# Mixer A's scores two tiles at a time, its values in the bank of turned q and k

## What is computed

```python
def diff_attention(q, k, v, lam):          # 4 heads, q and k of width 64 for each of 2 maps, v of width 128
    s = jnp.einsum('bhmqd,bhmkd->bhmqk', qb, k).astype(jnp.float32) * scale
    p = jax.nn.softmax(s, axis=-1)
    w = p[:, :, 0] - lam * p[:, :, 1]
    return jnp.einsum('bhqk,bhkd->bhqd', w.astype(v.dtype), v)
...
ya = diff_attention(qa, ka, va, lam)
ya = merge_heads(rms_norm(ya, subln_a) * (1.0 - lam_init))
```

## Time and profile before

| | |
|---|---|
| median of 3 runs | 2302.98 us (2302.33 to 2303.56) |
| profiled execution, first to last instruction | 2300.6 us |
| granted TensorE clock, mean | 0.999 |
| PE busy | 2263.2 us (98%) |
| PEld busy | 2125.2 us (92%) |
| DVE busy | 1720.5 us (75%) |
| ACT busy | 1116.4 us (49%) |

### The profile page before, as it was taken

One profiled execution on the slowest core, in us unless ns is written; L12 is line 12 of the kernel. 1 busy time (PEld: TensorE's weight loads), 2 busy tenths in 40 slices (PEclk: granted clock), 3 DMA queues, 4 the chain that ended last, 5 costly groups with the idle time before them and its releaser, 6 DMA issues.

```text
span 2300.6 us, 41723 instructions
## 1 busy us (share of the span) xinstructions
PE 2263.2 (98%) x15128; PEld 2125.2 (92%) x15128; DVE 1720.5 (75%) x4728; ACT 1116.4 (49%) x3059; POOL 58.3 (3%) x103
## 2 busy tenths in 40 slices
PE   7999999999999999999999999999999999999999
PEld 5888989999998999999888899899999989999998
DVE  7898888887886766677578867778887866676762
ACT  5667565444444444334357665754444353343340
POOL 0010120000000000000000102100000000000000
PEclk9999999999999999999999999999999999999999
DMA  7312321221111233322422111122111113332223
GB/s 287 116 48 68 113 91 70 96 94 61 56 51 45 80 113 121 101 99 66 161 81 82 55 64 48 55 84 88 74 42 51 48 52 104 108 119 92 90 94 115
DMA packets 78908, 200.28 MB, mean 87 GB/s; under 512 B 12272, under 2 KB 33392, under 8 KB 76912
## 3 DMA queue, kind: packets, MB, share of 16 engines
q1 hardware_dynamic: 62544, 171.87, 21.9%
q10 hardware_dynamic: 16160, 25.75, 3.1%
HBM read 176.59 MB, written 18.88 MB: 85 GB/s over the span
## 4 chain that ended last, share of the span: by engine, by line
PE 87%; DVE 7%; ACT 3%; issue 2%; DMA 0%; SPq 0%; DVEq 0%; ACTq 0%
PE ps_proj L1122 52%; PE ps_score L1166 12%; PE ps_pt L1166 9%; PE ps_pt L1315 2%; PE ps_score L1299 2%; PE ps_pv L1351 1%; PE ps_score L1283 1%; PE ps_pv L1332 1%; PE ps_tr L1365 1%; DVE top L2188 1%; PE ps_tr L1366 1%; PE ps_pv L1345 1%; ACT probs L1717 1%; PE ps_pt L1358 1%; ACT act_hi L1565 1%
## 5 line engine op out<-in xcount | busy, mean ns | idle before, releaser
L1122 PE MATMUL ps_proj<-w_hi,act_hi 128*128 128x384 f32 x1824 | 632.9, 347 | 4.8 <-DVE act_lo L2302 3.5
L1122 PE MATMUL ps_proj<-w_hi,act_lo 128*128 128x384 f32 x1824 | 612.7, 336 | 0.0
L1122 PE MATMUL ps_proj<-w_lo,act_hi 128*128 128x384 f32 x1824 | 612.4, 336 | 0.0
L1122 PEld LDWEIGHTS ps_proj<-w_hi,act_hi 128*128 128x128 f32 x1824 | 343.1, 188 | 9.4 <-ACT act_hi L1565 6.9
L1122 PEld LDWEIGHTS ps_proj<-w_lo,act_hi 128*128 128x128 f32 x1824 | 343.7, 188 | 0.0
L1122 PEld LDWEIGHTS ps_proj<-w_hi,act_lo 128*128 128x128 f32 x1824 | 343.0, 188 | 0.0
L1657 ACT ACTIVATE square<-ps_proj 128x256 f32<-128x256 f32 x228 | 88.1, 386 | 255.8 <-PE ps_proj L1122 255.5
L2121 DVE TENSOR_REDUCE ssq<-square 128x2 f32<-128x256 f32 (+1 forms) x228 | 95.5, 419 | 135.9 <-ACT square L1657 134.6
L2489 DVE TENSOR_TENSOR w_lo<-w_raw,w_hi 128x1536 fp32r<-128x1536 f32 (+3 forms) x105 | 169.6, 1616 | 13.3 <-ACT w_hi L1489 12.6
L1489 ACT ACTIVATE w_hi<-w_raw 128x1536 fp32r<-128x1536 f32 (+2 forms) x104 | 144.3, 1388 | 39.3 <-DVE merged L2470 18.3
L2398 DVE TENSOR_TENSOR s_lo<-s_raw,s_hi 128x512 fp32r<-128x512 f32 x224 | 150.8, 685 | 9.3 <-ACT s_hi L1820 7.5
(11 more groups left out here) (258 smaller groups left out, 5095.9 us busy)
## 6 DMA issues: line engine op xcount, KB each, us to landing
w_raw<-in_w SPq DMA_DIRECT2D x80, 768.0 KB, 5.7
s_raw<-in_w_gate SPq DMA_DIRECT2D x96, 256.0 KB, 3.2
strip<-in_w_strip SPq DMA_DIRECT2D x32, 512.0 KB, 6.5
w_raw<-in_w SPq DMA_DIRECT2D x24, 512.0 KB, 3.8
wb_raw<-in_w_branch SPq DMA_DIRECT2D x24, 512.0 KB, 3.8
first_ada<-in_w_first SPq DMA_DIRECT2D x8, 1024.0 KB, 13.0
w<-in_w_gate SPq DMA_DIRECT2D x32, 256.0 KB, 3.8
parked<-y_t ACTq DMA_DIRECT2D x4, 1536.0 KB, 5.1
```

The costliest lines, as they stand in the source:

```text
L1122: op = pe.matmul(out, sta[s](k), mov[m](k), start=(k == 0 and n == 0), stop=(k == chunks - 1 and n == 2))
```

## The change

Odd tiles of mixer A are scored one unit earlier, in the break of the even tile before them, right behind its scores (`steps`, `shared_scores`). They get two banks of their own, `ps_odd`, which are `ps_pt`'s second bank and the bank that was `ps_pv`; `ps_pt` now has three banks, and `ps_pv` is its third. Since `ps_odd` takes that bank, A's values go to columns 256 to 383 of the bank `ps_tr` (`valued`), and A's turned y to columns 384 to 511 (`turned_y`); turned q and k keep columns 0 to 255 of it.

PE's break is reordered for A: scores, then `turn_probs(a1)`, `values(a2)`, `turn_y(a3)`, `turn_unit(u2)`. A's `values` gets a wait for ACT to have read the q and k that were turned one unit earlier. `scores` of A now waits for the exponentials of the tile two before instead of one before; the first odd tile waits until DVE has read the projection of unit 5 from `ps_pt`.

ACT's iteration is reordered for A: `copy_probs(a1)` moves ahead of `exps(a0)`; `turn_out_y(a3)` moves from ahead of the exponentials to behind them, with a wait for the whole break's transposes; `y_rstds(a2)` moves to the end, behind `turn_out(u2)`. DVE's order is unchanged.

```diff
+def shared_scores(a):
+    return a[1] == "A" and a[3] % 2 == 1
...
         at = [n, n + 1, n + 2] * 2
+        if shared_scores(a):
+            at[0] = n - 1
...
-        ps_pt = pt("ps_pt", 2)
-        ps_pv = pt("ps_pv", 1)
+        ps_pt = pt("ps_pt", 3)
+        ps_pv, ps_odd = ps_pt[:, 1024:1536], ps_pt[:, 512:1536]
...
         def turned_y(a):
-            return ps_pt[:, 512:512 + P]
+            return ps_tr[:, 3 * P:4 * P] if a[1] == "A" else ps_pt[:, 512:512 + P]
+        def valued(a):
+            return ps_tr[:, 2 * P:3 * P] if a[1] == "A" else ps_pv[:, 0:P]
+        def scored(a):
+            return ps_odd if shared_scores(a) else ps_score[:]
...
             def scores(a):
-                if ATT_AT[a] and not second(a):
+                if a[1:] == ("A", 0, 1):
+                    pe.wait_ge(*dve_read.at(("q", l, "A", 0, 0, TILES - 1)))
+                elif kind == "A" and ATT_AT[a] and (h, t) != (0, 0):
+                    pe.wait_ge(*exp_ready.at(ATT[ATT_AT[a] - 2]))
+                elif ATT_AT[a] and not second(a):
...
             def values(a):
+                if kind == "A":
+                    pe.wait_ge(*turned_out.at(TURNED_BEFORE[("t", UNITS[AT_TILE[a]])]))
...
                 def between(k):
                         for a in SCORED.get(n, ()):
                             scores(a)
-                        if a3 is not None and a3[1] == "A":
-                            turn_y(a3)
                         for a in VALUED.get(n, ()):
-                            values(a)
+                            if a[1] != "A":
+                                values(a)
                         if a3 is not None and narrow(a3):
                             turn_y(a3)
                         for a in CROSSED.get(n, ()):
                             turn_probs(a)
+                        for a in VALUED.get(n, ()):
+                            if a[1] == "A":
+                                values(a)
+                        if a3 is not None and a3[1] == "A":
+                            turn_y(a3)
...
-                if a3 is not None and by_rows(a3):
+                if a3 is not None and narrow(a3):
                     turn_out_y(a3)
+                for a in COPIED.get(n, ()):
+                    if a[1] == "A":
+                        copy_probs(a)
                 for a in TOPPED.get(n, ()):
                     exps(a)
                 for a in TAKEN.get(n, ()):
+                    if not by_rows(a):
+                        take_y(a)
+                for a in COPIED.get(n, ()):
+                    if a[1] != "A":
+                        copy_probs(a)
+                if a3 is not None and a3[1] == "A":
+                    act.wait_ge(*turned_t.at(("t", u2)))
+                    turn_out_y(a3)
+                if u2 is not None and u2[0] == "q":
+                    turn_out(u2)
+                for a in TAKEN.get(n, ()):
                     if a[1] == "A":
                         y_rstds(a)
-                    elif not by_rows(a):
-                        take_y(a)
-                for a in COPIED.get(n, ()):
-                    copy_probs(a)
-                if u2 is not None and u2[0] == "q":
-                    turn_out(u2)
```

## The result

The changed kernel takes 2311.94 us (2310.56 to 2313.32, five runs) where the kernel before takes 2303.13 us on the same chip: 1.0037 times as long, 95% interval 1.0027 to 1.0048. It is 8.8 us slower; forecast were 8.0 (2311.0, range 2299 to 2316). A second five runs gave 2313.43 beside 2302.9 (1.0046, 1.0032 to 1.0060). The profiled execution has a span of 2311.5 us, 10.9 more than before; it was the slowest of its five runs, so sums made on this profile come out about 1.4 us above the median.

The account below looks back on a forecast made before the run. The loop of DVE and ACT was taken to bound layer 0, PE layer 1 by little. Layer 0's 6.8 us and layer 1's 1.2 made 8.0: span 2300.6 to 2308.6, plus 2.4 carried over, 2311.0 us, range 2299 to 2316.

Parts of the forecast that it names:

- The bound: DVE and ACT's loop sets layer 0's pace in units 12 to 23; PE sets layer 1's, by 0.5 us in 40.
- Part 1: Odd tiles of A scored with the tile before: 0.35 us less PE work each, 8.4 us in all.
- Part 2: ACT's new order: norm factor 0.60 us later, loop 2.4 us longer per six units in layer 0, 1.2 in layer 1.
- The start-up: First odd tile waits for DVE's read of unit 5's projection; 0.8 us put on the loop in each layer.
- the last units' terms: Units 24 to 29: 0.3 us added in layer 0, 1.0 us given back in layer 1.
- PE's saving counts: Rival: the loop has unseen slack, so the time falls by up to 8.4 us, to 2294.6; chance 0.14.
- The two cancel: Rival: DVE's lengthening, 3.6 us in layer 0, against half of layer 1's 4.2 us kept by PE: 2304.5 us; chance 0.16.
- A new wait ahead of the exponentials: Rival: ACT's copy waits for PE's values, even tiles' exponentials 0.3 to 1 us later, about 8 us more: 2319; chance 0.10.
- if ACT idles for L1728's wait on PE, the third rival holds: Sign in the profile after: ACT idling there would show A new wait ahead of the exponentials, about 8 us more.

Follow-up runs that it names:

- factor_late: Kernel before with only ACT's new order: copy of the probabilities ahead of the exponentials, y_t behind them, norm factor behind q and k; 2308.73 us.
- sample_pairs: Kernel before with only mixer A's tiles 4 and 5 scored in one run, in the banks they had; 2302.16 us.
- no_pairs: Changed kernel with no odd tile scored early, all else as in the change; 2307.29 us.
- first_apart: Changed kernel with the first odd tile of each layer scored in its own unit again; 2306.55 us.
- scale_late: Changed kernel with the first odd tile apart, and on DVE mixer A's scale_y moved behind w_lo and the dot product; 2304.0 us.

## Why the prediction was right, and where it was not

**The bound: right.** The loop of ACT and DVE sets the pace in layer 0. `factor_late` shows it from one side (PE untouched, 5.5 us slower), the pairs from the other: `sample_pairs` leaves the loop at 85.2 us, and 22 pairs take 7.7 us of work from PE for 0.7.

**Part 1: right in size.** In layer 1's break of the prompt pair the rows of before give 2.96 + 2.96 us for two tiles (from the last projection matmul ahead of a break to the first one behind), those of after 3.82 + 1.75, so 0.35 less; in `sample_pairs` the sample pair takes 2.97 + 1.54 where it took 2.53 + 2.32, 0.34 less.
**Part 2: right in place, more than a third too large (2.6 where 4.2 was forecast).** The factor is 0.54 us later behind the exponentials (forecast 0.60) and `y_tok` 0.41 (forecast 0.47). The first head takes 2.0 us more (forecast 2.4). The second takes 0.6 more (forecast 1.8): there the kernel before already needed 43.3 us, 1.4 more than for the first, with POOL at work. The forecast had allowed 0.6 us for that, and the `ssq` rows of the second head would have given 1.4. That POOL's work is what held it up, and that the later `y_tok` hides behind it, is argued and was not run by itself. Twelve iterations: 87.8 us against 89.5 forecast. In layer 1 six take 40.4 (forecast 40.7).

**The start-up: the mis-sized term.** "I put 0.8 us of it on the loop, an estimate between 0 and 1.6": measured 2.7 us a layer by the medians, 3.6 at the first `ssq` of layer 0 by the profile. I followed PE's delay only to the copy of the probabilities in unit 8. Ahead of it there is a closer listener: DVE's `qk` of iteration 6, which needs PE's late turn in unit 7 and had been ready at 68.2. PE's delay of 3 us was read rightly; who waits for the turn in unit 7 was not asked. The wait alone costs 2.1 us a layer. The fall of the clock, 1.6 us where it comes, was not in the sum at all.

So the forecast had the shares the wrong way round. It gave 1.6 us to the two starts and 6.4 to all the rest; measured are 5.4 and 3.4 by the medians (2311.94 - 2306.55, and 2306.55 against 2303.13). That 8.0 stands so close to 8.8 is partly luck.

**The sum by layers.** Layer 0 by the `ssq` rows: 3.6 at the start, 1.1 in units 7 to 11 (102.9 to 107.6 is 4.7 late), 2.0 and 0.6 in the two heads: 7.3 against 6.8 forecast (0.8 + 1.5 + 4.2 + 0.3), and after up to 8.9 in the units behind, it is 7.3 again from iteration 34 on, so units 24 to 29 cost nothing. Layer 1: 1238.5 to 1250.1 is 11.6 late, so the start and the units up to 12 cost 4.3 against 1.9 forecast; 1.1 in units 12 to 23, 1.8 given back by the end, where the profile is 10.9 late: 3.6 against 1.2. One term was too small by 2 to 3 us a layer, and the loop's and the last units' terms were too large by 2.3 in layer 0. Two more us of the 10.9 are not in the median: the run profiled after was 1.4 us above its median, and the one before, by its span, some 0.7 below.

**The rivals.** *PE's saving counts* is excluded by `no_pairs` against `first_apart`, and in layer 0 by `sample_pairs`. *The two cancel* had 2304.5 us, 7.4 below the measured time. *A new wait ahead of the exponentials* came, in layer 1 alone: 8.7 us before L1728 in seven places. It made the exponentials late in three of them, by 0.25, 0.23 and 1.46 us, and did not cost the 8 us of the rival, because ACT would have waited for the maxima meanwhile. By the prediction's own sign ("if ACT idles for L1728's wait on PE, the third rival holds") it would have held; the sign was too weak, since idling there costs only what it takes from the exponentials. Once `y_tok` is later still, as in `scale_late`, ACT idles there for up to 2.37 us, and about 0.8 us of that counts.

**Left open.** Whether the change would pay with a bank of its own for A's values was not tried: all eight banks are taken. As they share one with turned q and k, ACT's reads of q and k and DVE's read in `scale_y` have to come one after the other. The Trainium skill ("PSUM — Partial Sum Buffer", PSUM bank collisions raise a hardware error) says that two engines must not be in one bank at once and that the hardware doesn't wait for them; no run here shows that.

## What to carry to other kernels

When two engines wait for each other in a loop, find the longest chain around the loop before counting what a change takes off the third: 7.7 us less work for the engine at 98% was worth 0.7 us by the medians, and a small factor put half a microsecond later in each iteration, behind `y_t` and q and k, cost 7.8. When a change makes an engine stand once, list every instruction that waits for what it does next, the single-buffered ones first, and add what its clock may lose. A gain inside a change that loses can be worth running alone: the copy was, and with the sample pairs added it made the fastest kernel here.

## What the runs showed of the hardware

- PE's granted clock fell to 0.50 for about 3 us behind a standing of 1.96 or 2.21 us, in three of four cases, and matmuls of 128x384 stood 0.32 us apart instead of 0.173. With sixteen or eight transposes in the gap it stayed at 1.00, in four of four.
- Part of PE's waiting for a semaphore is not shown as idle: in one break it was 1.27 us longer and 0.82 of that was shown.
